# Norm weights multiplied into the projection weights of a hybrid attention block, roots applied behind the projections

## What is computed

```
h  = rms_norm(x, g_mix_norm);  z = h @ w_in
q, kc, vc, ksl, vsl, kwn, vwn, gate_logits, zu, zv = split(z)
q, ksl, kwn: rms_norm per head, rope;   kcmp, vcmp = gelu(blocks(kc or vc, + pe) @ w1) @ w2
o_attn = gates . (compressed, selected, window attention)      8 heads of 64
o_mix  = gelu(zu) * (tril(sp_w) @ rms_norm(gelu(zv)) + sp_b)
o = [rms_norm(o_attn, g_out[:512]), rms_norm(o_mix, g_out[512:])]
x = x + o @ w_out
h = rms_norm(x, g_ffn_norm)
x = x + square(relu(h @ w_ff1)) @ w_ff2
rms_norm(x, g) = x * rsqrt(mean(x * x) + eps) * g
```

## Time and profile before

| | us |
|---|---|
| median of 3 runs | 643.25 |
| lowest and highest | 639.94, 643.32 |
| the profiled execution | 643.82 |
| its span in the trace | 642.1 |
| TensorE busy | 631.1 |
| VectorE busy | 320.5 |
| ScalarE busy | 261.0 |
| GpSimd busy | 11.4 |

### The profile page before, as it was taken

How to read it: one execution, slowest core, us unless ns; L and a number is a source line. 1 busy time by engine, 2 the same in 40 slices (tenths; PEclk the granted TensorE clock), 3 DMA queues, 4 the chain that set the end, 5 groups by cost and what they waited for, 6 DMA issues and landing times.

```text
span 642.1 us, 8825 instructions
## 1 busy us (share of the span) xinstructions
PE 631.1 (98%) x3241; PEld 523.4 (82%) x3241; DVE 320.5 (50%) x499; ACT 261.0 (41%) x487; POOL 11.4 (2%) x30
## 2 busy tenths in 40 slices
PE   8999999999999899999999999999999999999997
PEld 7788787787888788888888888888888888888885
DVE  3797760677677577665333333333433333333323
ACT  4645671637455666544222222223322222222220
POOL 4000010000000000000000000000000000000000
PEclk9999999999999999999999999999999999999999
DMA  8321345441112010003232222222222222222103
GB/s 323 138 92 66 132 144 192 155 166 64 66 38 96 1 34 34 1 2 108 92 96 97 98 98 98 98 98 99 98 100 98 99 97 97 96 97 89 46 0 131
DMA packets 17229, 60.59 MB, mean 94 GB/s; under 512 B 2017, under 2 KB 2305, under 8 KB 17202
## 3 DMA queue, kind: packets, MB, share of 16 engines
q1 hardware_dynamic: 16416, 57.88, 25.1%
q0 software_dynamic: 784, 2.35, 1.1%
q10 hardware_dynamic: 2, 0.00, 0.0%
HBM read 58.12 MB, written 2.10 MB: 94 GB/s over the span
## 4 chain that ended last, share of the span: by engine, by line
PE 92%; DVE 3%; ACT 2%; issue 2%; POOL 0%; DVEq 0%; ACTq 0%; POOLq 0%
PE ps L320 25%; PE ps L322 25%; PE ps L321 25%; PE ps L1676 4%; PE ps L1664 2%; PE ps L1413 2%; PE ps L1621 1%; PE ps L1502 1%; PE ps L1622 1%; PE ps L1530 1%; PE ps L1641 1%; DVE ht_lo L976 1%; PE ps L1647 1%; PE ps L1602 1%; PE ps L1582 1%
## 5 line engine op out<-in xcount | busy, mean ns | idle before, releaser
L320 PE MATMUL ps<-ht_hi,w_hi_sb 128*128 128x512 f32 (+1 forms) x280 | 107.7, 385 | 0.0
L321 PE MATMUL ps<-ht_lo,w_hi_sb 128*128 128x512 f32 (+1 forms) x280 | 107.3, 383 | 0.0
L322 PE MATMUL ps<-ht_hi,w_lo_sb 128*128 128x512 f32 (+1 forms) x280 | 107.3, 383 | 0.0
L320 PE MATMUL ps<-w_hi_sb,a_hi 128*128 128x512 f32 x256 | 99.6, 389 | 0.0
L321 PE MATMUL ps<-w_lo_sb,a_hi 128*128 128x512 f32 x256 | 99.6, 389 | 0.0
L322 PE MATMUL ps<-w_hi_sb,a_lo 128*128 128x512 f32 x256 | 99.6, 389 | 0.0
L1289 DVE TENSOR_TENSOR w_lo_sb<-raw,w_hi_sb 128x1024 fp32r<-128x1024 f32 x64 | 78.3, 1225 | 9.9 <-ACT w_hi_sb L809 3.1
L320 PE MATMUL ps<-w_hi_sb,ht_hi 128*128 128x512 f32 x192 | 81.6, 425 | 1.3 <-DVE w_lo_sb L933 0.8
L322 PE MATMUL ps<-w_hi_sb,ht_lo 128*128 128x512 f32 x192 | 75.2, 392 | 0.0
L321 PE MATMUL ps<-w_lo_sb,ht_hi 128*128 128x512 f32 x192 | 75.0, 391 | 0.0
L1356 DVE TENSOR_TENSOR act_sb<-act_sb (+1 forms) x32 | 22.2, 692 | 102.8 <-ACT act_sb L891 102.8
(11 more groups left out here) (188 smaller groups left out, 810.6 us busy)
## 6 DMA issues: line engine op xcount, KB each, us to landing
raw<-in_w_ff SPq DMA_DIRECT2D x64, 512.0 KB, 3.5
raw<-in_w SPq DMA_DIRECT2D x24, 512.0 KB, 3.9
xs<-in_x SPq DMA_DIRECT2D x8, 512.0 KB, 6.1
raw<-in_cmp_w SPq DMA_DIRECT2D x8, 512.0 KB, 4.3
out_y<-xs SPq DMA_DIRECT2D x3, 512.0 KB, 2.6
raw<-in_w_c SPq DMA_DIRECT2D x4, 304.0 KB, 2.5
spw_sb<-in_sp_w POOLq DMA_DIRECT2D x1, 512.0 KB, 3.4
grow<-in_g_rows POOLq DMA_DIRECT2D x1, 512.0 KB, 6.7
```

The lines of the kernel that those rows point to most:

```text
L320: pe.matmul(out, l_hi, r_hi, start=start, stop=False)
L321: pe.matmul(out, l_hi, r_lo, start=False, stop=False)
L322: return pe.matmul(out, l_lo, r_hi, start=False, stop=stop)
```

## The change

The weights of the three norms are multiplied into the rows of w_in, w_out and w_ff1, and x, mix, attn and ffn rows are transposed as they are.

- The host passes the norm weights as columns, `g_cols` (128 x 3 x 8); ScalarE's queue loads them first. `hi` becomes two activations of 512 columns, each scaled by its block's column, and `lo` two scalar_tensor_tensor of 512 columns (raw times column minus high part).
- For w_ff1, GpSimd multiplies each raw unit in place by its columns ahead of `f_hi`, which now waits for `f_scaled`; w_ff2 is not scaled.
- The root of x is applied behind the input projection: as the scale of the activations that empty the tiles (`evac_q`, `evac_kv`, `evac_gelu`), by one multiplication of the gate logits, and for the transposed kc and vc by a row `rb`: VectorE makes a diagonal from the roots, TensorE multiplies ones by it (`scales`, behind the last tile of group A), VectorE copies it, and multiplies `par` in `blocks`.
- `norm_rows` is gone with its 20 calls (4 of x, 4 mix, 4 attn, 8 ffn), and so are the spreading products, `grow` and `grow_ffn`. Transposes wait for the load of x, for `mixed`, `o_evac` or `added`.
- GpSimd's seven table loads wait for x(3) instead of x(1). Fillers go from 12, 14, 20, 12 to 11, 6, 12. The order of ScalarE's and VectorE's streams in the first tiles is rewritten.

```diff
 SEQUENCE = [("x", 0), ("x", 1), ("out", "A", 0), ("x", 2), ("out", "A", 1), ("x", 3), ("out", "A", 2),
-            ("out", "A", 3), ("out", "B", 0), ("q", 0), ("out", "B", 1), ("q", 1),
+            ("out", "A", 3), ("rb",), ("out", "B", 0), ("q", 0), ("out", "B", 1), ("q", 1),
...
-WARM = 12, 14, 20, 12
-GROW_BANK = 2
+WARM = 11, 6, 12
...
-            pool.wait_ge(x_in[1], 16)
+            pool.wait_ge(x_in[NT - 1], 16)
...
-            pool.wait_ge(n_rows, NT)
-            pool.dma_start(grow[:, :], g_rows[1:2, :].broadcast_to([P, D])).then_inc(grow_out_in, 16)
-            pool.wait_ge(zv_norm, NT)
-            pool.dma_start(grow_ffn[:, :], g_rows[2:3, :].broadcast_to([P, D])).then_inc(grow_ffn_in, 16)
+            pool.wait_ge(gcol_in, 16)
+            with pool.Fori(0, NF // FR) as i:
+                for j in range(FR):
+                    pool.wait_ge(raw_in[j], i * 16 + (IN0 + 16))
+                    w = raw[:, j, :].rearrange("p (k n) -> p k n", k=NK)
+                    pool.tensor_tensor(w, w, bc(gcol_sb[:, 2, :].unsqueeze(2), [P, NK, P]), ALU.mult
+                                       ).then_inc(f_scaled, 1)
...
-                act.activation(w_hi_sb[:, n % HL, 0:width], raw[:, i % RAW, 0:width], ACT.Copy
-                               ).then_inc(w_hi, 1)
+                half = width // 2
+                for k in range(2):
+                    c = slice(k * half, k * half + half)
+                    act.activation(w_hi_sb[:, n % HL, c], raw[:, i % RAW, c], ACT.Copy, scale=gcol(n, k)
+                                   ).then_inc(w_hi, 1)
...
             def evac_q(t):
                 o = OUT["out", "A", t]
+                r = stat(rstd, "x", t)
+                act.wait_ge(n_rstd, t + 1)
                 wait_out(act, ("out", "A", t))
-                act.activation(o_sb[:, t, AW:], ps[:, o % 4, :], ACT.Square).then_inc(h_ssq, 1)
-                act.activation(o_sb[:, t, 0:AW], ps[:, o % 4, :], ACT.Copy).then_inc(out_evac, 1)
+                act.activation(o_sb[:, t, AW:], ps[:, o % 4, :], ACT.Square, scale=r).then_inc(h_ssq, 1)
+                act.activation(o_sb[:, t, 0:AW], ps[:, o % 4, :], ACT.Copy, scale=r).then_inc(out_evac, 1)
...
-                    f_hi(j, i * 16 + (IN0 + 32), i * FR + (NW + j + 1))
+                    f_hi(j, f_scaled, i * FR + (FR + j + 1), i * FR + (NW + j + 1))
...
+                i, half = SPLITS[n], width // 2
+                r = raw[:, i % RAW, 0:width].rearrange("p (k n) -> p k n", k=2)
+                h, l = slot_w(n, w_hi_sb, half), slot_w(n, w_lo_sb, half)
+                for k in range(2):
+                    dve.wait_ge(w_hi, 2 * n + k + 1)
+                    c = slice(0, half)
...
+                    last = dve.scalar_tensor_tensor(out=l[:, k, c], in0=r[:, k, c], scalar=gcol(n, k),
+                                                    in1=h[:, k, c].bitcast(F32), op0=ALU.mult, op1=ALU.subtract)
+                last.then_inc(w_lo, 1)
...
+            x_lo(3, 1)
             dve.wait_ge(tables_in, 16 * 7)
-            head_sum(0)
             rotate(0)
-            x_lo(3)
             stack_lo(0)
-            lo(5)
-            head_sum(1)
             rotate(1)
             lo(6)
             stack_lo(1)
             lo(7)
+            j = FILL["rb", 0]
+            wait_fill(dve, j)
+            for odd in range(2):
+                rows = slice(HD * odd, HD * odd + HD)
+                last = dve.tensor_copy(rb[rows, :], ps[rows, fill_bank(j), odd::2])
+            last.then_inc(free[j % 4], 1)
...
                 dve.wait_ge(out_evac, OUT["cmp_in", kv] + 1)
+                wait_free(dve, FILL["rb", 0])
+                dve.tensor_tensor(par[:, kv, :, :], par[:, kv, :, :], bc(rb[:, :].unsqueeze(1), [P, NKV, SEQ // 2]),
+                                  ALU.mult).then_inc(par_scaled, 1)
...
-            norm_rows("mix", 0)
-            norm_rows("mix", 1)
             mix(2)
...
-                    pe.wait_ge(n_rows, ROWN[kind, t, 0 if kind == "x" else i] + 1)
+                    if kind == "x":
+                        pe.wait_ge(x_in[t], 16)
+                    elif kind == "mix":
+                        pe.wait_ge(mixed, t + 1)
+                    elif kind == "attn":
+                        pe.wait_ge(o_evac, 2 * t + 2)
+                    else:
+                        pe.wait_ge(added, ADD_NO["attno", t, i] + 1)
...
-                    if g == "A" and u == (3, 2, 1, None)[t]:
+                    if g == "A" and u == (2, 2, 1, None)[t]:
                         rows_t("x", t + 1)
...
+            def scales():
+
+                j = FILL["rb", 0]
+                wait_bank(pe, j)
+                pe.wait_ge(ident_made, 3)
+                pe.wait_ge(diag_made, 1)
+                pe.matmul(ps[:, fill_bank(j), :], ones[:, :], diag[:, :, :].rearrange("p t s -> p (t s)"),
+                          start=True, stop=True).then_inc(filled, 1)
```

More of the change, by code:

```diff
@@ L282, in hybrid_block @@
         spw_made, pads_made = sem("spw_made"), sem("pads_made")
-        n_ssq, n_root, n_rstd, n_rows = [sem(f"n_{k}") for k in ("ssq", "root", "rstd", "rows")]
+        n_ssq, n_root, n_rstd = [sem(f"n_{k}") for k in ("ssq", "root", "rstd")]
+        f_scaled = sem("f_scaled")
         ht_half, ht_done = sem("ht_half"), sem("ht_done")
@@ L617, in x_norm, with x_hi @@
                 norm_root("x", t)
-            def x_hi(t):
-                ht_hi_evac("x", t, 0)
-                ht_hi_evac("x", t, 1)
+            def x_hi(t, i):
+                ht_hi_evac("x", t, i)
+            x_hi(0, 0)
+            act.wait_ge(gcol_in, 16)
+            hi(0)
+            x_hi(0, 1)
+            hi(1)
             x_norm(0)
-            hi(0)
-            x_hi(0)
-            hi(1)
+            hi(2)
+            x_hi(1, 0)
+            x_hi(1, 1)
+            hi(3)
             x_norm(1)
-            hi(2)
-            hi(3)
-            x_hi(1)
+            evac_q(0)
             x_norm(2)
+            stats_root(0, 0)
+            hi(4)
+            x_hi(2, 0)
+            x_hi(2, 1)
             x_norm(3)
-            hi(4)
-            x_hi(2)
-            hi(5)
-            evac_q(0)
-            stats_root(0, 0)
-            x_hi(3)
-            stack_hi(0)
             evac_q(1)
             stats_root(0, 1)
+            hi(5)
+            x_hi(3, 0)
+            x_hi(3, 1)
+            stack_hi(0)
             hi(6)
@@ L1043, in stack_lo @@
                                       ).then_inc(st_lo, 1)
-            x_rows(0)
+            x_lo(0, 0)
+            dve.wait_ge(gcol_in, 16)
             lo(0)
-            x_lo(0)
+            x_lo(0, 1)
             lo(1)
-            x_rows(1)
+            norm_inv("x", 0)
             lo(2)
+            x_lo(1, 0)
+            x_lo(1, 1)
             lo(3)
-            x_lo(1)
-            x_rows(2)
-            x_rows(3)
+            norm_inv("x", 1)
+            head_sum(0)
+            norm_inv("x", 2)
             lo(4)
-            x_lo(2)
+            x_lo(2, 0)
+            x_lo(2, 1)
+            norm_inv("x", 3)
+            dve.wait_ge(n_rstd, NT)
+            dve.wait_ge(ident_made, 2)
+            dve.tensor_tensor(diag[:, :, :], bc(ident[:, :].unsqueeze(1), [P, NT, P]),
+                              bc(stat(rstd, "x", 0, NT).unsqueeze(2), [P, NT, P]), ALU.mult).then_inc(diag_made, 1)
+            head_sum(1)
+            lo(5)
+            x_lo(3, 0)
+            x_lo(3, 1)
             dve.wait_ge(tables_in, 16 * 7)
-            head_sum(0)
             rotate(0)
-            x_lo(3)
             stack_lo(0)
-            lo(5)
-            head_sum(1)
             rotate(1)
@@ L1110, in _ @@
             dve.tensor_tensor(glog[:, :, :], glog[:, :, :], parts[:, :, 1, :], ALU.add).then_inc(free[j % 4], 1)
+            wait_free(dve, j)
+            dve.tensor_tensor(glog[:, :, :], glog[:, :, :], bc(stat(rstd, "x", 0, NT).unsqueeze(2), [P, NT, 3 * NH]),
+                              ALU.mult).then_inc(g_step, 1)
             blocks(0)
@@ L1226, in _ @@
             row_max(1)
-            norm_rows("mix", 2)
-            norm_rows("mix", 3)
             for i in range(2):
@@ L1630, in first_scores @@
                     scores(v)
-            RUN = {"x": lambda t: rows_t("x", t), "out": output, "q": stack_t, "k": lambda t: stack_t(NT + t),
+            RUN = {"x": lambda t: rows_t("x", t), "rb": scales, "out": output, "q": stack_t, "k": lambda t: stack_t(NT + t),
                    "gate": gate, "gateT": gate_back, "cmp_in": cmp_in, "sp": spatial, "hid": hidden, "hidT": hidden_t,
@@ L1643, in _ @@
             warm(WARM[0], 1)
-            pe.wait_ge(ident_made, 3)
-            pe.wait_ge(grow_in, 16)
-            for b in range(2):
-                pe.matmul(ps[:, GROW_BANK + b, :], ones_row[:, :], grow_row[:, b * 512:b * 512 + 512],
-                          start=True, stop=True).then_inc(grow_spread, 1)
-            warm(WARM[1], 1)
             for s in SEQUENCE:
```

151 lines of the change are left out of this document (53 added, 98 removed).

## The result

The changed kernel takes **640.93 us** (median of 16 runs, 639.57 to 642.20) against 643.31 for the kernel before (16 runs on the same chip, 639.94 to 645.68). The ratio is 0.996, 95% interval 0.9943 to 0.9977: by it 2.6 us less (2.4 between the medians), where 6.05 were forecast. The times of the kernel before lie in three groups, near 640.0, 643.5 and 645.5 us, so places in the traces are the finer measure: the last product starts at 634.25 instead of 637.23, 2.98 us earlier.

What follows compares the result with a forecast made beforehand. TensorE, busy 98% of the span, was taken as the bound, its start waiting for VectorE's scaling of x(0). Terms -6.1 + 0.9 - 0.2 - 0.3 - 0.35 + 0 = -6.05 gave 637.8, stated as 637.2 us; range 634 to 641.5.

Steps and rivals of the forecast that it cites:

- Rival 1: Start gives back half: first tile's products partly at TensorE's lower clock level, 2 to 3 us lost, 640 left; chance 13%.
- rival 3: VectorE becomes the bound between 28 and 60 us, unit 7 late by 2 us more, result 641; chance 7%.
- First product at 8.5: Start: the first projection product can start at 8.5 us instead of 14.83.
- Second tile at 16.6, "-6.1": Start: the second output tile begins at 16.6 us instead of 22.73, 6.1 us less.
- Unit 3's wait: First tile: products of unit 2 end at 13.8, VectorE finishes unit 3 at 15.2, the tile ends at 16.6.
- Group B, "-0.2": First tile of group B: stall of 0.2 us for unit 7 against about 0.4 before, so 0.2 less.
- Product of ones, +0.9: New 128x512 fp32 product of ones with a diagonal, 0.88 us, adding 0.9 on TensorE's path.
- Mix, -0.3: Middle: mix transposes wait only for the products once row scalings go; 0.3 us less (0 to 0.8).
- last feed-forward wait, -0.35: End of attention: the 0.25 us wait for the last feed-forward row scaling goes, with its latency 0.35 less.
- Attention, 0: Attention stage: VectorE loses eight instructions, VectorE and ScalarE gain split time; taken as equal, 0 (-0.6 to +0.6).
- a weaker form: Of the GpSimd rival (5% in all): VectorE slows while GpSimd works; at most 1 us in the attention stage.
- GpSimd, 0 on the path: Feed-forward: GpSimd's 32 multiplications take 2.4 us each, hidden while under TensorE's 5.43 per unit; cost 0.

Runs made afterwards that it cites:

- e1: The changed kernel with 24 instead of 6 fillers between the transposes of x(0) and the first product; 639.13 us, ratio 0.9941 to the kernel before.
- e2: The changed kernel with VectorE's low halves of units 6 and 7 ahead of the second rotation; 638.25 us, ratio 0.9929 to the kernel before.
- e3: The changed kernel without GpSimd's multiplications of the 32 feed-forward units (that norm weight missing from the result); 638.81 us, ratio 0.9935 to the kernel before.
- e7: The changed kernel with GpSimd multiplying each feed-forward unit once more, into a buffer nobody reads; 644.64 us, ratio 1.0022 to the kernel before.

## Why the prediction was wrong

The sign and the place were right, and the time fell inside the range of 634 to 641.5, near its upper end; but it lies outside the forecast's own 635 to 639.5 and not below 640.0, to which 78% were given. It is in the range because that was stretched to take in rivals 1 and 3, with their 640 and 641. The gain was forecast at 6.05 us and is 2.6 by the runs, 2.98 by the last product. The places below are those of the profiled executions; how the shortfall divides in the others is not known, and twelve of the sixteen do not have the clock's part. By the forecast's own steps:

- **First product at 8.5**: 9.06. The steps were right within 0.4 each (ScalarE's copy at 5.67 for 5.3, its split pair 1.32 for 1.1), and their sum 0.6.
- **Second tile at 16.6, "-6.1"**: 18.93, -3.80. *This step failed.* It priced the products of units 0 and 1 at 0.23, 2.8 us; they took 4.46 (9.06 to 13.52), most of it at a granted clock of 0.50: 1.7 lost. The pause ahead of them was forecast as "a microsecond" and measured 2.06; e1 fills it and the twelve take 2.86. Rival 1 had this, with "2 to 3 lost" and 640 left, at a chance of 13%. It deserved more: the forecast itself put a pause where the kernel before had twenty fillers. Its argument against (5.9 us of unbroken transposes are enough) concerned the rise of the pace, and took work to begin at 7.8 where the trace has TensorE busy from 1.62 on. The rise did come early, the six fillers of 6.18 took 0.82 us, and the pause undid it. Unit 3's wait was forecast (13.8 to 15.2) and came so: 1.5.
- **Group B, "-0.2"**: measured +1.15. From the transposes of x(3) to the first q stack 2.02 us are lost, 0.87 of them by the product of ones. *The second failure.* TensorE's waits of 0.52 and 0.27 cost 1.1 with the slower starts behind them, and e2 removes them; with it the place comes out at -0.2. Of the 0.4 us that I had inferred for the kernel before from a count of products its trace shows 0.2, a late start at 45.19. The backlog came from the order (rotation before units 6 and 7), as e2 shows; 0.8 us of it is the multiplication stretched from 0.69 to 1.47 beside GpSimd's select, whose share in TensorE's waits was not tried by itself. It is rival 3 in a small form, and it is in the executions without the fall of the clock too: e2's take 638.0 to 638.4, those of the changed kernel 639.6 and more.
- **Product of ones, +0.9**: 0.87 on TensorE's path (its row says 1.02, but from 37.05 to 38.38 are 1.33 us, and two products alone take 0.46). Right.
- **Mix, -0.3**: -0.43 (from the first q stack to the compressed probabilities), and **last feed-forward wait, -0.35**: -0.42 from the end of attention on. Right.
- **Attention, 0**: -0.44. e3 shows the two parts: -1.0 from the relief of VectorE, +0.56 from GpSimd. Inside the bounds, but for a reason that the forecast had only as "a weaker form".
- **GpSimd, 0 on the path**: right for the feed-forward. 2.4 us per unit was taken, 2.04 measured, and up to 4.7 (e7) the period of TensorE stays. The Trainium skill's GPSIMD Engine Reference, section 3.1, gave an estimate of 2.3 us; the trace agrees within 0.3. Its section 1, that the two engines share their access to SBUF for VectorE's instructions with two SBUF inputs, is what e3 and e7 show: 745 to 1420 ns with both inputs in SBUF, 680 unchanged with one in PSUM.

Adding up: forecast 6.05, less 1.7 (clock), less 0.6 (first product), less 1.35 (group B), plus 0.6 (mix, attention, feed-forward) is 3.0, and the trace has 2.98.

## What to carry to other kernels

Fillers on TensorE are part of a start's timing in both directions: too many stand in the path (eight of the kernel before cost 1.6 us), too few leave a pause that lowers the clock for the products behind it (1.6 us in an execution that has the fall). When a change moves the start, size them anew, so that they end just where the first product can begin. Work given to GpSimd is free only where VectorE has slack: here it cost nothing in the feed-forward and 0.56 us in the attention stage. A profile is one execution: ahead of crediting a loss in it to every run, look whether the timed executions bear the same sign. And a backlog on VectorE is read from its order: what TensorE wants next goes ahead of what it wants later.
